# Prompt sparse attention: the order of transpositions, scores and values on TensorE

## The chip, the cores and the metric

The kernel runs on one core of a Trainium2 chip. The metric is the time of one execution in microseconds on the device, the median of several runs.

## What is computed

One inference step of a decoder layer for a prompt of 1024 tokens and 32 sample tokens, all in float32. The change lies in the prompt's native sparse attention. For 8 query heads in 2 key groups, cut to what matters:

```python
s = einsum(q, k) * DH ** -0.5 - slope * dist      # masked where not valid
e = exp(s - max(s)); p = e / sum(e)
# three branches over blocks of 128 queries:
#   compressed: up to 63 compressed keys (63 = 1024 // 16 - 1)
#   selected:   the 16 best blocks of 64 keys, here all causal keys
#   window:     the last 512 keys
o_a = g0 * o_compressed + g1 * o_selected + g2 * o_window
```

`g0` to `g2` are sigmoid gates. The rest of the layer (projections, a state-space mixer, dilated attention, cross attention, a feed-forward network) isn't touched.

## The kernel before

The program is a row of stages. A stage is a call of `together`, which takes lanes. A lane holds one generator per engine and a number of steps, and `together` writes the lanes' instructions engine by engine in an order set by numbers: step k of a lane that starts at `start` and takes `length` stands at `start + (k + 0.5) * length / steps`. So the order on each engine is fixed when the program is built, and lanes meet on an engine only in that order.

The stage of this case has four lanes: `dense.lane(36)`, start 0, length 1; `nsa_prompt_lane`, start 0.08, length 0.92; `branch_weights_lane`, start 0.3, length 0.3 (a few small operations); and `copies_lane`, which issues cache copies from ScalarE. The dense lane has 36 units of 8 steps, so 288, and a step is one gate matmul at L288 (two records in the trace, 352 columns); after a unit ScalarE or VectorE copies its output (L308). Matmuls in float32 show as two records each, transpositions as one.

`nsa_prompt_lane` first turns (transposes) 12 loaded groups of query and key rows (L644, `nsap_raw`; the loads are issued at L847 by SyncE, four groups deep). Then it has 32 attention steps s: 4 query heads r per key group times 8 query blocks i. A step works on both key groups g at once:

- **score** (L658): matmuls of `q_T` and `k_T` into the two buffers `nsap_S`, one per key group, in units of at most 512 columns. Units of step s+2 are made during step s.
- **bias** (L764, VectorE): adds the distance table, writes `nsap_probs`, and takes the maximum into `nsap_tops`; it releases the `nsap_S` buffer for the next unit. After the last unit `shift` (L775 to L778) makes `nsap_neg`.
- **exp** (L731, ScalarE): the exponential of a branch of step s+1, with its sum.
- **weight** (L784 to L791, VectorE): six multiplications of step s+1's probabilities by gate over sum.
- **turn_probs** (L644, TensorE): four (or two) transpositions of a group of `nsap_probs` into `nsap_T0` or `nsap_T1`; **copy_probs** (L706 on ScalarE, L708 on VectorE) takes them to `nsap_probs_T`, four groups deep, by the group's parity.
- **values** (L677): matmuls with `nsap_v` or `nsap_vcs` into `nsap_O`; after a step's last group ScalarE copies it to `nsap_oa` (L749).

A group is two 128-key tiles of both key groups, or the compressed keys. Step i has 2, 3, 4, 5, 6, 7, 7, 8 groups. `subs(s)` says how many sections (turns between which other lanes come) a step has. Section j of TensorE holds unit j of step s+2, the turn of group j and the values of group j-1:

```python
for j in range(subs(s)):
    if j < n_units(s + 2):
        score(s + 2, j)
    if j < n_groups(s):
        turn_probs(s, j)
    if 1 <= j <= n_groups(s):
        values(s, j - 1)
    yield
```

Of the kernel before, what the change touches and what calls it, by code (L numbers as in the profile page):

```python
# [23 lines left out]
P = 128  # L24
# [520 lines left out]
def nsa_prompt_lane(nc, st, ins, proj, kc_T, vc, oa_T, ident):  # L545
# [39 lines left out]
    def n_cmp(i):  # L585
        return min(NCMP_P, (i + 1) * P // CMP_S - 1)

    def units(i):
# [8 lines left out]
        out, width = [], 512  # L597
        for part in sel + win + [("cmp", 0, n_cmp(i), TX + 8 * (PT - 1 - i), CX, 4)]:
# [32 lines left out]
    def subs(s):  # L631
        return max(n_units(s + 2), n_groups(s) + 1, 3)
# [6 lines left out]
    def pe_program(pe):  # L639
# [49 lines left out]
        for s in range(2):  # L689
            for j in range(n_units(s)):  # L690
                score(s, j)
            yield
        for s in range(n):
            for j in range(subs(s)):
                if j < n_units(s + 2):
                    score(s + 2, j)
                if j < n_groups(s):
                    turn_probs(s, j)
                if 1 <= j <= n_groups(s):
                    values(s, j - 1)  # L700
                yield

# [13 lines left out]
    def copy_probs(eng, s, j, side):  # L716
        group = group0[s] + j
        if j < n_groups(s) and group % 2 == side:
# [6 lines left out]
    def act_program(act):  # L725
# [14 lines left out]
        yield  # L740
        for s in range(n):
            for j in range(subs(s)):
                copy_probs(act, s, j, 0)
                if s + 1 < n and j < 3:
                    exp(s + 1, (1, 2, 0)[j])
                if j == subs(s) - 1:
                    r, i = steps[s]
                    act.wait_ge(pv, group0[s + 1] - group0[0])
                    act.copy(oa[:, r, i * P:(i + 1) * P], O[s % 2][:, :]).then_inc(out_made, 1)  # L749
                yield  # L750

    def dve_program(dve):
# [51 lines left out]
        for s in range(n):  # L804
            for j in range(subs(s)):
                copy_probs(dve, s, j, 1)
# [4 lines left out]
                if j == subs(s) - 1 and s + 1 < n:  # L811
                    weight(s + 1)
                yield

    def pool_program(pool):
# [11 lines left out]
        for s in range(n):  # L827
# [5 lines left out]
            for _ in range(subs(s)):  # L833
                yield
# [4 lines left out]
    def sp_program(sp):  # L839
# [26 lines left out]
        for s in range(n):  # L866
# [4 lines left out]
            for _ in range(subs(s)):  # L871
                yield
# [4 lines left out]
    return Lane(len(preps) + 2 + sum(subs(s) for s in range(n)), pe_program, act_program, dve_program, pool_program, sp_program)  # L877
# [3243 lines left out]
```

## Time and profile before

| | before |
|---|---|
| median of 3 runs | 3273.9 us |
| lowest and highest run | 3272.72, 3279.45 us |
| profiled execution: span | 3273.0 us |
| TensorE busy | 3015.6 us, 92% |
| VectorE busy | 1257.5 us, 38% |
| ScalarE busy | 640.6 us, 20% |
| DMA | 344.79 MB, mean 105 GB/s |

The profile is of one execution. The span runs from its first to its last instruction; what lies around it is not in the table, since the times of the runs were taken apart. In the views PE is TensorE's matmuls and PEld its weight loads, DVE is VectorE, ACT ScalarE, SP SyncE, and a "q" behind an engine is its queue of waits and DMA issues. Idle time stands with what ended it. Matmuls are pipelined, so the time of a matmul in a stream is read from one start to the next.

### The profile page before, as it was taken

Reading aid. Unit: us, or ns where it says so; the run is one execution under the profiler, and the core shown is the slowest. Engines: PE = TensorE matmul, PEld = TensorE weight load, DVE = VectorE, ACT = ScalarE, POOL = GpSimd, SP = SyncE. Lnnn points to the kernel's source line nnn. Section 1 sums busy time; section 2 is a strip of 40 time slices with the busy share of each in tenths; the row PEclk is TensorE's granted clock in tenths of the full one; section 3 lists DMA queues with packets and bytes.
Section 4 is the critical chain, followed back from the end, with each engine's and each line's share of the span. In section 5 each row is a group of like instructions: output and inputs, shape, how many; then the busy total and the mean of one; then the engine's idle time right before and its main releaser. Section 6 shows DMA issues by size and latency. Waiting matters only on the chain. (4 is left out here: it accounts for less than half of the span.)

```text
span 3273.0 us, 42944 instructions
## 1 busy us (share of the span) xinstructions
PE 3015.6 (92%) x15198; PEld 2004.1 (61%) x15198; DVE 1257.5 (38%) x2963; ACT 640.6 (20%) x1529; POOL 469.3 (14%) x351
## 2 busy tenths in 40 slices
PE   7999999989997899699899899899699999989998
PEld 5777777665555565454554565455488888874443
DVE  3111123225642675255555343133456656550000
ACT  2111000002220333233333221144311111110000
POOL 0001000004301432100000100011122332220000
PEclk8999999999998889899999999899799999999999
DMA  7544253428854432621110444200143333404010
GB/s 171 118 95 103 75 166 112 146 84 231 254 160 129 147 103 65 181 69 36 40 32 33 142 138 156 94 15 33 55 141 110 121 136 108 141 22 158 34 34 26
DMA packets 336639, 344.79 MB, mean 105 GB/s; under 512 B 60945, under 2 KB 305361, under 8 KB 335078
## 3 DMA queue, kind: packets, MB, share of 16 engines
q1 hardware_dynamic: 296730, 262.54, 27.6%
q10 hardware_dynamic: 39734, 79.98, 7.2%
q8 instruction: 103, 1.69, 0.2%
q14 instruction: 72, 0.59, 0.1%
HBM read 289.11 MB, written 110.01 MB: 122 GB/s over the span
## 5 line engine op out<-in xcount | busy, mean ns | idle before, releaser
L284 PE MATMUL d_ps<-d_w,mixer_u_T 128*128 128x288 f32 (+2 forms) x2048 | 610.8, 437 | 15.9 <-PEq L145 10.3
L284 PEld LDWEIGHTS d_ps<-d_w,mixer_u_T 128*128 128x128 f32 x2048 | 375.4, 195 | 150.4 <-issue 47.9
L288 PE MATMUL d_ps<-mixer_u_T,d_w 128*128 128x352 f32 x1152 | 428.9, 498 | 24.4 <-ACT d_ob L308 13.8
L2923 PE MATMUL down_ps<-down_w,feed_g_T 128*128 128x512 f32 x704 | 305.4, 596 | 8.4 <-DMA down_w<-ffn_w_down 8.4
L288 PEld LDWEIGHTS d_ps<-mixer_u_T,d_w 128*128 128x128 f32 x1152 | 206.4, 199 | 131.8 <-issue 70.1
L2923 PEld LDWEIGHTS down_ps<-down_w,feed_g_T 128*128 128x128 f32 x704 | 134.4, 191 | 177.7 <-issue 168.5
L3133 PE MATMUL ffn_ps<-up_u_T,up_up_w 128*128 128x264 f32 x704 | 165.2, 394 | 6.3 <-DMA ffn_state<-state_ffn_conv 6.3
L3133 PE MATMUL ffn_ps<-up_u_T,ffn_S 128*128 128x264 f32 x704 | 163.8, 386 | 0.0
L3133 PE MATMUL ffn_ps<-ffn_T,up_up_w 128*128 128x264 f32 x704 | 163.8, 386 | 0.0
L308 DVE COPY d_ob<-d_ps 128x288 f32<-128x288 f32 (+3 forms) x144 | 66.4, 462 | 233.0 <-PE d_ps L284 158.3
L3133 PEld LDWEIGHTS ffn_ps<-up_u_T,up_up_w 128*128 128x128 f32 x704 | 133.8, 193 | 29.5 <-issue 6.7
L3133 PEld LDWEIGHTS ffn_ps<-up_u_T,ffn_S 128*128 128x128 f32 x704 | 133.8, 190 | 22.9
L3133 PEld LDWEIGHTS ffn_ps<-ffn_T,up_up_w 128*128 128x128 f32 x704 | 133.8, 190 | 22.9
L2763 PE MATMUL mix_B<-gates_o_T,mix_wb 128*128 128x352 f32 x480 | 144.1, 464 | 0.0
L3483 PE MATMUL tail_ps_a<-feed_g_T 128*128 128x512 f32 (+1 forms) x288 | 135.9, 622 | 6.1 <-DVE tail_y_a L3513 4.2
L2763 PEld LDWEIGHTS mix_B<-gates_o_T,mix_wb 128*128 128x128 f32 x480 | 92.1, 192 | 51.5 <-issue 1.5
L1320 PE MATMUL cmp_H<-cmp_rows_T,cmp_w 128*128 128x254 f32 (+1 forms) x576 | 122.6, 373 | 0.0
L3189 DVE TENSOR_TENSOR ffn_h<-ffn_kept,ffn_ps 128x264 f32<-128x264 f32 (+2 forms) x220 | 76.3, 372 | 120.6 <-PE ffn_ps L3133 117.8
L3252 DVE SCALAR_TENSOR_TENSOR ffn_c<-ffn_h,ffn_now,ffn_c 128x1072 f32<-128x1072 f32 x88 | 117.5, 1335 | 3.1
L764 DVE CUSTOM_DVE_ANT_0 nsap_probs<-nsap_S,nsap_scaled 128x128 f32<-128x128 f32 (+11 forms) x256 | 99.7, 435 | 43.6 <-PE nsap_S L658 43.6
L708 DVE COPY nsap_probs_T<-nsap_T 128x512 f32<-128x512 f32 (+4 forms) x84 | 53.6, 639 | 162.1 <-PE nsap_T L644 159.7
L1320 PEld LDWEIGHTS cmp_H<-cmp_rows_T,cmp_w 128*128 128x128 f32 x576 | 106.9, 196 | 14.3
(467 smaller groups left out, 3783.0 us busy)
## 6 DMA issues: line engine op xcount, KB each, us to landing
out_dil_sample<-cache_dil_w ACTq DMA_DIRECT2D x10, 3264.0 KB
up_up_w<-ffn_w_up SPq DMA_DIRECT2D x44, 512.0 KB, 5.1
cmp_rows<-cache_nsa_kv SPq DMA_DIRECT2D x128, 128.0 KB
graw<-d_ob SPq DMA_DIRECT2D x72, 176.0 KB
mix_gate<-graw SPq DMA_DIRECT2D x24, 528.0 KB, 6.0
dils_qb<-proj SPq DMA_DIRECT2D x24, 512.0 KB, 6.9
d_w<-w_in SPq DMA_DIRECT2D x24, 512.0 KB, 5.4
ssd_x<-proj SPq DMA_DIRECT2D x29, 384.0 KB, 4.8
```

Source lines behind the costliest of these rows:

```text
L284: mm = pe.matmul(self.ps[u % 2][0:rows, 0:cols], self.u_T[:, k, r0:r0 + rows], self.view(i)[:, k, :], start=(k == 0), stop=(k == DK - 1))
L288: mm = pe.matmul(self.ps[u % 2][:, 0:cols], self.view(i)[:, k, x, :], self.u_T[:, k, c * third:(c + 1) * third], start=(k == 0), stop=(k = ...
L308: copy(self.ob[0:rows, u % ring, 0:cols], self.ps[u % 2][0:rows, 0:cols]).then_inc(self.copied[u % 2], 1)
L708: eng.tensor_copy(out, src).then_inc(copied[1], 1)
L764: mm = dve.tensor_tensor_reduce(probs[:, s % 3, g, p0:p0 + b - a], S[g][:, col:col + b - a], scaled[:, r % 2, g, c0:c0 + b - a], 1.0, -3.0 ...
L1320: mm = pe.matmul(H[s][:, :, 0:blocks], w1[:, s, l, :], rows_T[:, r0:r0 + (KVH - 1) * LP + 1:LP, j:j + blocks], start=(l == 0), stop=(l == ...
L2763: mm = pe.matmul(B[u % BANKS][:, 0:third], wb[:, s, k, :], o_T[:, k, c * third:(c + 1) * third], start=(k == lo), stop=(k == hi - 1))
L2923: mm = pe.matmul(ps[i % ring][:, 512 * h:512 * (h + 1)], lhs_T[:, k, r0:r0 + m], w[:, k, 512 * h:512 * (h + 1)], start=(k == 0), stop=(k = ...
L3133: mm = pe.matmul(bank(p, x)[:, 0:quarter], lhs(slot)[:, k, :], rhs(x)[:, k, :], start=(k == 0), stop=(k == KH - 1))
L3189: dve.tensor_tensor(out, a, b, ALU.add).then_inc(summed, 1)
L3252: dve.scalar_tensor_tensor(out, row[:, k:k + conv], now[:, k, a:a + 1], out, ALU.mult, ALU.add).then_inc(convolved, 1)
L3483: mm = pe.matmul(ps_a[0:m, 512 * h:512 * (h + 1)], mix_T[:, k, r0:r0 + m], w_out[:, k, 512 * h:512 * (h + 1)], start=(k == 0), stop=(k == ...
```

## The change

- `units` packs a step's parts by size: the parts are sorted, the widest first, and each goes into the first unit with room. There are 88 units in all where there were 96.
- A section of TensorE now holds two groups' transpositions, then one score unit, then the values of both groups of the section before. `sections(s)` is the largest of the units of s+2, the pairs of groups, and 3.
- ScalarE does two of the three branches' exponentials in section 1, and the output copy (`take_out`) moves to the section in which the step's last values are made, which may be the first of the next step.
- VectorE weights step s+1 in the last section ahead of that section's biasing.
- The lane has 127 steps where it had 214.

```diff
+        for part in sorted(sel + win + [("cmp", 0, n_cmp(i), TX + 8 * (PT - 1 - i), CX, 4)], key=lambda x: x[1] - x[2]):
             m = part[2] - part[1]
-            if width + m > 512:
-                out.append([])
-                width = 0
-            out[-1].append((width, part))
-            width += m
+            for unit in out:
+                col, last = unit[-1]
+                at = col + last[2] - last[1]
+                if at + m <= 512:
+                    unit.append((at, part))
+                    break
+            else:
+                out.append([(0, part)])
...
-    def subs(s):
-        return max(n_units(s + 2), n_groups(s) + 1, 3)
+    def sections(s):
+        return max(n_units(s + 2), n_pairs(s), 3)
+    def n_pairs(s):
+        return (n_groups(s) + 1) // 2
+    def whole_at(s, j):
+        if j == 0 and s >= 1 and n_pairs(s - 1) == sections(s - 1):
+            return s - 1
+        return s if j == n_pairs(s) else None
+    def pair_of(s, j):
+        return range(2 * j, min(2 * j + 2, n_groups(s)))
...
+        before = []
         for s in range(n):
-            for j in range(subs(s)):
+            for j in range(sections(s)):
+                for x in pair_of(s, j):
+                    turn_probs(s, x)
                 if j < n_units(s + 2):
                     score(s + 2, j)
-                if j < n_groups(s):
-                    turn_probs(s, j)
-                if 1 <= j <= n_groups(s):
-                    values(s, j - 1)
-                yield
+                for x in before:
+                    values(*x)
+                before = [(s, x) for x in pair_of(s, j)]
+                yield
...
+            for j in range(sections(s)):
+                for x in pair_of(s, j):
+                    copy_probs(act, s, x, 0)
+                if s + 1 < n and j < 2:
+                    for br in ((1,), (2, 0))[j]:
+                        exp(s + 1, br)
+                if whole_at(s, j) is not None:
+                    take_out(whole_at(s, j))
+                yield
...
+                for x in pair_of(s, j):
+                    copy_probs(dve, s, x, 1)
+                if j == sections(s) - 1 and s + 1 < n:
+                    weight(s + 1)
                 if j < n_units(s + 2):
                     bias(s + 2, j)
                     if j == n_units(s + 2) - 1:
                         shift(s + 2)
-                if j == subs(s) - 1 and s + 1 < n:
-                    weight(s + 1)
                 yield
```

How the order moves, on TensorE, in the middle of step s=4 (i=4). Before:

```order
L658 MATMUL nsap_S<-nsap_k_T,nsap_q_T 128x512 x2
L644 MATMUL nsap_T<-const_ident,nsap_probs 128x128 x4
L677 MATMUL nsap_O<-nsap_probs_T,nsap_v 64x128 x4
L288 MATMUL d_ps<-mixer_u_T,d_w 128x352
L658 MATMUL nsap_S<-nsap_k_T,nsap_q_T 128x128 x2
L658 MATMUL nsap_S<-nsap_kc,nsap_q_T 128x55 x2
L644 MATMUL nsap_T<-const_ident,nsap_probs 128x128 x4
L677 MATMUL nsap_O<-nsap_probs_T,nsap_v 64x128 x4
L288 MATMUL d_ps<-mixer_u_T,d_w 128x352
L644 MATMUL nsap_T<-const_ident,nsap_probs 128x128 x4
L677 MATMUL nsap_O<-nsap_probs_T,nsap_v 64x128 x4
L288 MATMUL d_ps<-mixer_u_T,d_w 128x352
```

And now, where L661 is the transposition, L675 the score, L694 the values (counts here are matmuls of the program):

```order
L661 MATMUL nsap_T<-const_ident,nsap_probs 128x128 x8
L675 MATMUL nsap_S<-nsap_k_T,nsap_q_T 128x512 x2
L694 MATMUL nsap_O<-nsap_probs_T,nsap_vcs 64x128 x2
L694 MATMUL nsap_O<-nsap_probs_T,nsap_v 64x128 x4
L288 MATMUL d_ps<-mixer_u_T,d_w 128x352 x2
L661 MATMUL nsap_T<-const_ident,nsap_probs 128x128 x8
L675 MATMUL nsap_S<-nsap_k_T,nsap_q_T 128x384 x2
L675 MATMUL nsap_S<-nsap_k_T,nsap_q_T 128x128 x2
L694 MATMUL nsap_O<-nsap_probs_T,nsap_v 64x128 x8
L288 MATMUL d_ps<-mixer_u_T,d_w 128x352 x3
L675 MATMUL nsap_S<-nsap_kc,nsap_q_T 128x55 x2
L694 MATMUL nsap_O<-nsap_probs_T,nsap_v 64x128 x8
```

Each section had its own run of four transpositions and of four value matmuls; now eight stand together, twice as many gate matmuls follow, and the units of 512, 128 and 55 columns and of 384 columns are cut as 384 with 128, and 55 alone.

On VectorE, at the end of step s=3 (i=3). Before:

```order
L775 TENSOR_TENSOR nsap_tops<-nsap_tops 128x2x2
L777 TENSOR_SCALAR nsap_neg<-nsap_tops 128x2x2
L778 TENSOR_SCALAR nsap_neg<-nsap_tops 128x2
L708 COPY nsap_probs_T<-nsap_T 128x512
L784 SCALAR_TENSOR_TENSOR nsap_rs<-nsap_sums,nsap_eg 128x6
L786 RECIPROCAL nsap_rs<-nsap_rs 128x6
L791 TENSOR_SCALAR nsap_probs<-nsap_probs,nsap_rs 128x39 x2
L791 TENSOR_SCALAR nsap_probs<-nsap_probs,nsap_rs 128x640 x4
L764 ISA nsap_probs,nsap_tops<-nsap_S,nsap_scaled 128x512
L764 ISA nsap_tops 128x1
```

And now, with the weighting at L814 to L821 and the biasing at L794:

```order
L730 COPY nsap_probs_T<-nsap_T 128x512
L814 SCALAR_TENSOR_TENSOR nsap_rs<-nsap_sums,nsap_eg 128x6
L816 RECIPROCAL nsap_rs<-nsap_rs 128x6
L821 TENSOR_SCALAR nsap_probs<-nsap_probs,nsap_rs 128x39 x2
L821 TENSOR_SCALAR nsap_probs<-nsap_probs,nsap_rs 128x640 x4
L794 ISA nsap_probs,nsap_tops<-nsap_S,nsap_scaled 128x256
L794 ISA nsap_tops 128x1
L794 ISA nsap_probs,nsap_tops<-nsap_S,nsap_scaled 128x128
L794 ISA nsap_tops 128x1
```

The biasing and the shift of step 5's last unit stood ahead of the weighting of step 4; now the weighting follows the section's copy directly and the biasing comes behind it.

## Rows read from the trace of the kernel before

**Rows 1.** The page of the profile, its first part: busy time by engine.
```profile
PE 3015.6 (92%) x15198; PEld 2004.1 (61%) x15198; DVE 1257.5 (38%) x2963; ACT 640.6 (20%) x1529; POOL 469.3 (14%) x351
```

**Rows 2.** Windows: us, then each engine's busy time, granted clock, DMA share, GB/s.
```profile
1310.00:1860.00 550.00, 479.31 (x2960) 272.96 (x2960) 258.16 (x966) 183.53 (x533) 26.94 (x9) 0.97 0.22 65
...
1430.00:1460.00 30.00, 28.13 (x193) 16.13 (x194) 17.61 (x57) 9.95 (x26) 6.73 (x2) 1.00 0.10 31
...
1580.00:1590.00 10.00, 8.65 (x45) 5.62 (x46) 4.88 (x21) 7.59 (x16) 0.00 (x0) 0.66 0.48 125
```

**Rows 3.** Groups by line, 1325:1855: shapes, count | busy us, mean ns | idle before, releasers.
```profile
L644 PE MATMUL nsap_T<-const_ident,nsap_probs 128*128 128x128 f32 (+7 forms) x592 | 97.6, 283 | 3.4 <-DVE nsap_probs L791 3.4
L677 PE MATMUL nsap_O<-nsap_probs_T,nsap_v 128*64 128x128 f32 x1056 | 87.9, 286 | 4.0 <-ACT nsap_probs_T L706 3.6 <-DVE nsap_probs_T L708 0.4
L658 PE MATMUL nsap_S<-nsap_k_T,nsap_q_T 64*128 64x512 f32 (+3 forms) x384 | 83.0, 514 | 28.9 <-DVE nsap_tops L764 28.5
...
L658 PE MATMUL nsap_S<-nsap_kc,nsap_q_T 64*128 64x7 f32 (+7 forms) x128 | 11.5, 247 | 11.1 <-DVE nsap_tops L764 11.1
L644 PE MATMUL nsap_T<-const_ident,nsap_raw 128*128 128x128 f32 x48 | 9.8, 341 | 14.7 <-DMA nsap_raw<-proj 13.7 <-ACT nsap_k_T L706 1.0
```

**Rows 4.** Time line of PE: start, us, line, names, shapes, count [idle before].
```profile
1433.78 0.60 PE L644 MATMUL nsap_T<-const_ident,nsap_probs 128*128 128x128 f32 x4
1434.31 0.66 PE L677 MATMUL nsap_O<-nsap_probs_T,nsap_v 128*64 128x128 f32 x8
1434.90 0.86 PE L288 MATMUL d_ps<-mixer_u_T,d_w 128*128 128x352 f32 x2
1435.59 0.60 PE L644 MATMUL nsap_T<-const_ident,nsap_probs 128*128 128x128 f32 x4
...
1439.47 1.13 PE L658 MATMUL nsap_S<-nsap_k_T,nsap_q_T 64*128 64x512 f32 x4
1440.53 0.42 PE L644 MATMUL nsap_T<-const_ident,nsap_probs 128*47 128x128 f32 x2
...
1442.19 1.13 PE L658 MATMUL nsap_S<-nsap_k_T,nsap_q_T 64*128 64x512 f32 x4 [0.66 <-DVE nsap_tops L764]
1443.26 0.66 PE L644 MATMUL nsap_T<-const_ident,nsap_probs 128*128 128x128 f32 x4
1443.84 0.44 PE L677 MATMUL nsap_O<-nsap_probs_T,nsap_vcs 47*64 47x128 f32 x4
1444.21 0.86 PE L288 MATMUL d_ps<-mixer_u_T,d_w 128*128 128x352 f32 x2
```

**Rows 5.** The same view of PE while the loaded rows are transposed.
```profile
1353.03 0.76 PE L288 MATMUL d_ps<-mixer_u_T,d_w 128*128 128x352 f32 x2
1353.62 0.60 PE L644 MATMUL nsap_T<-const_ident,nsap_raw 128*128 128x128 f32 x4
1354.06 1.35 PE L288 MATMUL d_ps<-mixer_u_T,d_w 128*128 128x352 f32 x4
```

**Rows 6.** Time line of DVE over the end of the same step.
```profile
1436.30 0.69 DVE L708 COPY nsap_probs_T<-nsap_T 128x512 f32<-128x512 f32 x1 [1.70 <-PE nsap_T L644]
...
1437.32 2.38 DVE L791 TENSOR_SCALAR nsap_probs<-nsap_probs,nsap_rs 128x47 f32<-128x47 f32 x6
1440.74 0.69 DVE L764 CUSTOM_DVE_ANT_0 nsap_probs<-nsap_S,nsap_scaled 128x512 f32<-128x512 f32 x1 [1.03 <-PE nsap_S L658]
```

**Rows 7.** Groups of DVE by form, 1370:1850: one weighting of two widths.
```profile
L791 DVE TENSOR_SCALAR nsap_probs<-nsap_probs,nsap_rs 128x640 f32<-128x640 f32 x40 | 19.8, 547 | 0.0
...
L791 DVE TENSOR_SCALAR nsap_probs<-nsap_probs,nsap_rs 128x1024 f32<-128x1024 f32 x8 | 5.6, 747 | 0.0
```

**Rows 8.** Time lines of SP's queue and of PE at the first steps.
```profile
1343.92 12.06 SPq L847 DMA_DIRECT2D nsap_raw<-proj  x14
...
1370.50 0.61 PE L658 MATMUL nsap_S<-nsap_kc,nsap_q_T 64*128 64x15 f32 x4 [4.43 <-DVE nsap_tops L764]
```

**Rows 9.** Time line of PE at the longest wait inside the loop.
```profile
1581.35 0.70 PE L677 MATMUL nsap_O<-nsap_probs_T,nsap_v 128*64 128x128 f32 x4 [3.56 <-ACT nsap_probs_T L706]
```

More of the change, by code:

```diff
@@ L692, in pe_program @@
             yield
+        before = []
         for s in range(n):
[L694 removed]
+            for j in range(sections(s)):
+                for x in pair_of(s, j):
+                    turn_probs(s, x)
                 if j < n_units(s + 2):
                     score(s + 2, j)
[L697 to L700 removed]
+                for x in before:
+                    values(*x)
+                before = [(s, x) for x in pair_of(s, j)]
                 yield
+        for x in before:
+            values(*x)
+        yield
     def copy_group(eng, group, out, src):
@@ L717, in copy_probs @@
         group = group0[s] + j
-        if j < n_groups(s) and group % 2 == side:
+        if group % 2 == side:
             pairs = blocks(steps[s][1])[j]
@@ L740, in act_program, with take_out @@
         yield
+        def take_out(s):
+            r, i = steps[s]
+            act.wait_ge(pv, group0[s + 1] - group0[0])
+            act.copy(oa[:, r, i * P:(i + 1) * P], O[s % 2][:, :]).then_inc(out_made, 1)
         for s in range(n):
[L742 to L749, printed above, removed]
+            for j in range(sections(s)):
[6 more added lines that the diff above has]
+                    take_out(whole_at(s, j))
                 yield
+        if n_pairs(n - 1) == sections(n - 1):
+            take_out(n - 1)
+        yield
     def dve_program(dve):
@@ L804, in dve_program @@
         for s in range(n):
-            for j in range(subs(s)):
-                copy_probs(dve, s, j, 1)
+            for j in range(sections(s)):
+                for x in pair_of(s, j):
+                    copy_probs(dve, s, x, 1)
+                if j == sections(s) - 1 and s + 1 < n:
+                    weight(s + 1)
                 if j < n_units(s + 2):
@@ L832, in pool_program @@
                 scale(r + 1)
-            for _ in range(subs(s)):
+            for _ in range(sections(s)):
                 yield
@@ L870, in sp_program @@
                 sp.dma_start(oa_T[r - 1], oa[:, r - 1, :]).then_inc(stored, 16)
-            for _ in range(subs(s)):
+            for _ in range(sections(s)):
                 yield
@@ L875, in sp_program @@
         sp.wait_ge(stored, 16 * NSA_R)
-    return Lane(len(preps) + 2 + sum(subs(s) for s in range(n)), pe_program, act_program, dve_program, pool_program, sp_program)
+    return Lane(len(preps) + 2 + 1 + sum(sections(s) for s in range(n)), pe_program, act_program, dve_program, pool_program, sp_program)
 def dil_prompt_lane(nc, st, ins, proj, o_dil, od_T, ident):
```

3 lines of the change are left out of this document (1 added, 2 removed).

## The prediction

> **What bounds the kernel now.** The page first: TensorE is busy for 92% of the span and no other engine for more than 38% [rows 1]. So the questions are how long the stage that the change touches lasts, and what TensorE does there. The windows give its place: from about 1327 us (first transposition of nsap_raw) to 1849.5 us; of the 550 us that hold it TensorE shows 479 busy, VectorE 258, ScalarE 184, the DMA engines 22% [rows 2]. In the first 60 us TensorE waits for loads; afterwards it is busy for 26 to 29 of every 30 us at a granted clock of 1.00, as in 1430:1460.
>
> The groups by line then say what ends the idle time [rows 3]: 40.0 us before score matmuls (28.9 + 11.1), for VectorE's biasing of the unit before; 14.7 us before the transpositions of loaded rows, for DMA; 3.4 us for the weighting; 4.0 us before value matmuls, 3.6 of it a single event. That is 47.4 us without the loads.
>
> The time line of TensorE shows a second loss, which counts as busy [rows 4, 5]. Four transpositions (T) take 0.44 us from start to start if a gate matmul (D) follows, 0.53 us if values (V) follow: 0.09 for leaving. One D (two records) takes 0.59 us after a T, 0.70 after a V (0.69 in the rounded rows): 0.11 for entering. I take 0.09 for leaving a D too. A V of 8 records takes 0.59 us and one of 4 takes 0.37: 0.055 for a record, so 0.15 us of any V run is fixed. A 512-wide score unit (S) takes 1.06 us against 0.85 at D's rate of 0.59 us per 352 columns: 0.20. T after S takes 0.58 where T after D takes 0.53: 0.05. T and D have the same shape of weights, 128*128, S has 64*128 and V 128*64; with like shapes nothing is lost, with every other neighbour about 0.16 us.
>
> **The change, part by part.** No matmul, copy, exponential or byte is removed or added; only order and waits move.
>
> *Fewer changes of shape.* I counted runs of one kind from the first transposition of the stage to its end in the built order. Before there are 657 runs: 170 D entered from V or S (0.11 each, 18.7 us), 127 D left to S or V (0.09, 11.4), 95 S runs (0.20, 19.0), 93 T after S (0.05, 4.7), 136 T left to V (0.09, 12.2) and 168 V runs (0.15, 25.2): 91.2 us. After there are 406: 111 entered (12.2), 19 left (1.7), 87 S (17.4), no T after S, 92 T left (8.3), 92 V (13.8): 53.4 us. The difference is **-38 us**. Two neighbours, T before S and S before V, are nearly absent before; I take leaving and entering as above, and bound each at 0.05 either way, +-7 us over some 137 of them.
> The Trainium skill, in TensorEngine Tiling (Array Packing), Key Properties, says that a change of tiling mode drains the engine. Read as a wait until the last matmul has ended (the 283 ns that a transposition takes), the 236 changes removed would be worth 67 us and the time would be 3176 us; the start-to-start times above have no room for that, and the measured 0.16 us decides.
>
> *Score units wait for less.* Now a unit is biased in one section and the next is scored after only V and one D, while VectorE needs 2.72 us from a 512-wide unit's start to its release: 1.27 us until it begins, two biasings of 0.65, 0.15 to wake TensorE [rows 4, 6]. After the change S, V8, D2, T8 stand between (numbers now count the program's matmuls: V4 is 8 records, a second V4 adds 0.44): 1.05 + 1.03 + 1.29 + 0.96 = 4.3 us. VectorE's copy of the section lies within the 1.27 us, so inside a step these waits go. The packing by size takes 96 units down to 88, so 8 fewer such waits; it moves no column.
>
> *A new wait at the end of a step.* VectorE now weights step s+1 in the last section ahead of that section's biasing, behind its copy, and TensorE's next transpositions need it; then the next score needs the biasing behind it. A weighting takes 2.7 us from the copy's end [rows 6], for widths 768, 640 and 47; two widths' durations [rows 7] give 0.067 us for 128 columns, so 3.0 for step i=7, 2.85 for 6, 2.6 for 4. The copy starts 0.71 us after the first transposition and takes 0.69 [rows 4, 6]. Step by step, TensorE's path from the last T to the next against VectorE's, without and with a copy of its own:
> i=6: T4 0.53 + V8 1.03 + D2 1.29 = 2.85, against 0.7 (1.4) + 3.0 + 0.15 = 3.85 (4.55): 1.0 to 1.7 us lost.
> i=3: with a 431-column unit 3.8 against 3.45 (4.15), and then two biasings, taken at the 0.65 us of 512 columns, before the next score: 0.4 to 1.0.
> i=5: two transpositions alone, 3.15 against 3.5 (4.0): 0.35 to 0.85. i=7 and 0: 0 to 0.5. i=1, 2, 4 have a last section without transpositions, which covers it: 0.
> The middles make 3.1 us a round of eight steps, 12.4 us for four. Behind the waiting transposition stand on TensorE the gate matmuls, which nobody needs soon. I keep the first steps' wait of 4.43 us [rows 8] (it hangs on the chain bias, exponential, weighting of step 0, which isn't touched) and the 4.0 us before values, though their cover grows. Stalls: 47.4 - 12.4 - 4.4 - 4.0, **-27 us**. Bounds: boundaries 0 to 25 us (twice the middles), -39 to -14.
>
> *ScalarE* gets two branches' exponentials in a section (about 2.4 us with the longest copy 3.0) against sections of 3 to 4.3 us, and its output copy moves up to a section later; O is double-buffered, so the cost is nothing. Should ScalarE be late, T would wait for its buffer first.
>
> *Loads.* The lane's 214 turns become 127 beside the same 288 gate matmuls, so each gets 2 or 3 D instead of 1 or 2; the twelve turns with loads get ten D more. SyncE issues the loads in its order: 14 between 1343.92 and 1355.98 us [rows 8], so they land no earlier; but the waits take in gate matmuls. The ten D are 5.9 us; from 0 to 9 us of the 14.7 [rows 3]: **-4.5 us**.
>
> The sum: -38 - 27 - 4.5 = -69 us. The profiled execution has a span of 3273.0 us, the median of the three runs is 3273.9, so against the median **3205 us**, 2.1% less.
>
> **The rivals.**
> *The boundary costs more.* If VectorE's tail takes 1.75 us at all 31 boundaries, 54 us, the gain is 38 + 4.5 + 47.4 - 54 - 8.4 = 27 us: 3246 us. For it: everything that VectorE does is in one queue, and the copy ahead of the weighting waits for TensorE itself. Against it: four of eight steps have the spare section or little to weight. Chance 0.12.
> *Waits inside a run.* Each run of T8 or V8 holds a semaphore wait in its middle; 76 joins of T and 76 of V. If each stops the early load of weights, at the 0.11 us that D pays for it: 17 us, 3222 us. Against it: a T with a wait behind a D costs nothing now (0.59). Chance 0.08.
> *The clock (slower than before).* Around the 3.56 us wait that ends at 1581.35 us [rows 9] the window 1580:1590 has a granted clock of 0.66 [rows 2], 6.8 us at 1.2 GHz in place of 2.4: 3.4 us of work lost. If every boundary, with its wait and a run of transpositions on either side, did the same, 31 x 3.4 = 105 us: 3310 us, slower; it decides from 20 drops on. Against it: the window 1430:1460 has 1.00 [rows 2] though TensorE waits in it (0.66 us at 1442.19 [rows 4]). Chance 0.04.
> The Trainium skill, in TensorE: Matmul & The Clock Gate, Part 4, PE-mode transpose, says that transpositions don't count as busy for the clock, which speaks against gathering them; the trace, where that window has transpositions in every turn and 1.00, shows no sign of it so far.
> *The change does nothing.* If gate matmuls and not the waits set the pace, all would move and nothing shrink: 3274 us. The 40 us of named waits speak against it. Chance 0.02.
>
> **How the numbers follow.** My forecast has 0.74. Its own bounds: gains of 31 + 14 + 0 = 45 to 45 + 39 + 9 = 93, the ends unlikely together. With the joins inside and the boundary rival half inside, 3186 to 3240 us. Faster than before by over 0.2% (about what a measurement can tell here, 6.5 us): 0.94; within: 0.02; slower: 0.04.
>
> **What would show it.** After: idle before the score matmuls under 15 us, before transpositions for the weighting 8 to 15 us, in steps i=6, 3 and 5; 406 runs with the same start-to-start prices (T8 before S 0.96 us, V8 before D 1.03); the last value matmul about 1780 us; loads' waits about 10 us; granted clock 1.00 in the stage's windows. I am wrong if T before S or S before V costs over 0.25 us, if idle before transpositions passes 30 us, or if windows fall below 0.9.

## The result, and the profile after

The changed kernel has a median of 3198.5 us (3192.5 to 3199.9, four runs), the kernel before on the same chip 3275.1 us: a ratio of 0.976 [0.9744, 0.9776], 76.6 us less. Forecast were 3205 us and 69 us less; the range held the time. A second measurement of the same kernel beside the experiments gave 0.977 [0.9748, 0.9792]. One execution, of e5 below, took 8313.6 us at a mean granted clock of 0.57 and is left out of its median.

The page of the changed kernel, the span and the busy times, which answer to [rows 1]:

```profile
span 3198.0 us, 42937 instructions
...
PE 2970.8 (93%) x15198; PEld 2010.5 (63%) x15198; DVE 1260.8 (39%) x2963; ACT 639.6 (20%) x1529; POOL 469.7 (15%) x351
```

The count of matmuls is the same, 15198, yet TensorE's busy time fell by 44.8 us: what a change of shape costs is counted as busy, as the prediction had read it, and so is what the lower clock costs (both are taken apart below). The other 30 us of the span's 75.0 were idle time. The windows of the stage, with the columns of [rows 2], show how full TensorE is now:

```profile
1310.00:1790.00 480.00, 443.04 (x2970) 284.49 (x2972) 261.40 (x969) 182.98 (x534) 29.33 (x11) 0.97 0.26 77
...
1430.00:1460.00 30.00, 29.38 (x214) 19.14 (x214) 21.26 (x71) 13.31 (x34) 6.73 (x2) 1.00 0.10 18
```

In 1430:1460 it was busy for 28.13 us with 193 matmul records; now for 29.38 with 214. The groups by line from 1325 to 1780 us answer to [rows 3]:

```profile
L661 PE MATMUL nsap_T<-const_ident,nsap_probs 128*128 128x128 f32 (+7 forms) x592 | 80.7, 275 | 7.3 <-DVE nsap_probs L821 6.6 <-DVE nsap_probs_T L730 0.6
L694 PE MATMUL nsap_O<-nsap_probs_T,nsap_v 128*64 128x128 f32 x1056 | 78.0, 281 | 0.0
L675 PE MATMUL nsap_S<-nsap_k_T,nsap_q_T 64*128 64x512 f32 (+3 forms) x384 | 77.9, 499 | 2.3 <-DVE nsap_tops L794 2.3
L675 PE MATMUL nsap_S<-nsap_kc,nsap_q_T 64*128 64x7 f32 (+7 forms) x128 | 11.4, 253 | 4.4 <-DVE nsap_tops L794 4.4
L661 PE MATMUL nsap_T<-const_ident,nsap_raw 128*128 128x128 f32 x48 | 9.2, 325 | 12.8 <-DMA nsap_raw<-proj 12.8
```

The waits before scores went from 40.0 to 6.7 us, and 4.4 of those are the single wait at the first steps. The waits before values are gone. Those of the transpositions for the weighting rose from 3.4 to 6.6 us; those for loads hardly moved, 13.7 to 12.8.

**The stage by its parts.** The same reading was made of every kernel below, from the first transposition of nsap_raw to the last value matmul. The columns are the stage's length; the number of runs of one kind in the order, and their price by the prediction's start-to-start prices (91.2 and 53.4 us there; a sum over every neighbour gives 90.4 and 52.9, and this one sum is used for all kernels); TensorE's waits before scores, before transpositions for the weighting, for loads, and before values; and the time in it at the lower clock of 1.2 GHz. All in us except the runs.

Each row is read from one profiled execution. The whole times of one kernel differ by up to 18 us from run to run, and the profiled execution was the fastest or nearly the fastest of its kernel for e3, e5 and e7 and the slowest for e2b and e8, so small differences between rows, those at 1.2 GHz above all, may be of the execution and not of the kernel. The changed kernel was profiled twice: its stage took 447.5 and 447.6 us, with 23.9 us at 1.2 GHz both times.

| kernel | stage | runs | price | scores | weighting | loads | values | at 1.2 GHz |
|---|---|---|---|---|---|---|---|---|
| before | 521.8 | 657 | 90.4 | 39.9 | 3.4 | 13.7 | 4.0 | 34.1 |
| after | 447.5 | 406 | 52.9 | 6.7 | 6.6 | 12.8 | 0 | 23.9 |
| e1_turn_first | 499.0 | 657 | 83.4 | 12.9 | 14.4 | 13.2 | 3.2 | 30.7 |
| e7_units_only | 509.4 | 649 | 87.7 | 35.9 | 3.4 | 11.6 | 4.0 | 23.9 |
| e8_branch_spread | 524.4 | 657 | 90.4 | 38.8 | 6.8 | 13.4 | 0.8 | 41.0 |
| e2b_alternate | 463.7 | 512 | 67.6 | 4.7 | 9.1 | 12.8 | 0 | 27.3 |
| e3_old_units | 449.7 | 422 | 56.1 | 4.4 | 7.1 | 13.1 | 0 | 23.9 |
| e4_weight_behind | 496.8 | 406 | 52.9 | 4.4 | 47.9 | 13.6 | 0 | 47.8 |
| e5_weight_ahead | 439.7 | 406 | 52.9 | 4.8 | 1.6 | 13.5 | 0 | 23.9 |

Before to after: price -37.5, waits for VectorE and ScalarE from 47.3 to 13.3, -34.0, loads -0.9, and 10.2 us less at half speed, worth half of that if TensorE had work throughout, -5.1 (an estimate). That makes -77.5 us; the stage shrank by 74.3, and of the span's 75.0 all but 0.7 lies in it. Two small waits stand in no column: the 1.0 us for ScalarE's copy of nsap_k_T [rows 3] is gone, and 0.6 us for VectorE's copy to nsap_probs_T is new.

### The profile page after: what moved, and what is told of

Its sections match the earlier page's. It is cut to its first block and busy times, and to the rows that moved or that the text cites. A ratio compares the mean times of both kernels' runs of the same rounds, so it can differ in the third digit from the quotient of the medians.

```text
span 3198.0 us, 42937 instructions
## 1 busy us (share of the span) xinstructions
PE 2970.8 (93%) x15198; PEld 2010.5 (63%) x15198; DVE 1260.8 (39%) x2963; ACT 639.6 (20%) x1529; POOL 469.7 (15%) x351
## 3 DMA queue, kind: packets, MB, share of 16 engines
q8 instruction: 103, 1.69, 0.2%
## 5 line engine op out<-in xcount | busy, mean ns | idle before, releaser
L288 PE MATMUL d_ps<-mixer_u_T,d_w 128*128 128x352 f32 x1152 | 404.3, 489 | 24.8 <-ACT d_ob L308 14.2
L794 DVE CUSTOM_DVE_ANT_0 nsap_probs<-nsap_S,nsap_scaled 128x512 f32<-128x512 f32 (+11 forms) x256 | 99.5, 438 | 39.9 <-PE nsap_S L675 39.9
L753 ACT ACTIVATE nsap_probs<-nsap_probs,nsap_neg 128x640 f32<-128x640 f32 (+9 forms) x192 | 112.6, 589 | 11.4 <-DVE nsap_neg L808 11.4
```

The source lines that it names most:

```text
L288: mm = pe.matmul(self.ps[u % 2][:, 0:cols], self.view(i)[:, k, x, :], self.u_T[:, k, c * third:(c + 1) * third], start=(k == 0), stop=(k = ...
L753: act.activation(x, x, ACT.Exp, scale=DH ** -0.5, bias=neg[:, s % 3, g, br:br + 1], accum_out=sums[:, s % 3, g, br:br + 1]).then_inc(exped, 1)
L794: mm = dve.tensor_tensor_reduce(probs[:, s % 3, g, p0:p0 + b - a], S[g][:, col:col + b - a], scaled[:, r % 2, g, c0:c0 + b - a], 1.0, -3.0 ...
```

## The experiments

Ten edits, most of them one piece of code each, were made from the kernel before or from the changed one; the ratio is always to the kernel before on the same chip, in runs beside it.

**e1: the order of a section alone.** From the kernel before: transpositions ahead of the score, four at a time, and nothing else.

```diff
+                if j < n_groups(s):
+                    turn_probs(s, j)
                 if j < n_units(s + 2):
                     score(s + 2, j)
-                if j < n_groups(s):
-                    turn_probs(s, j)
                 if 1 <= j <= n_groups(s):
                     values(s, j - 1)
```

> The kernel before, still one group a section, with the transpositions ahead of the score unit instead of behind it. My theory: what ends the waits before scores is that transpositions, values and a gate matmul lie between a score unit and the next while VectorE's copy no longer stands behind the score: 1.06 + 0.59 + 0.69 + 0.53 = 2.9 us against the 2.72 us that VectorE needs. Idle before score matmuls falls from 40.0 to about 12 us, the changes of shape cost 83 us instead of 90, so about 35 us less than before: 3240 us. Rival: the waits go only with two groups and two gate matmuls in a section; then only the 7 us of shapes are gained: 3268 us.

Measured: 3245.0 us, 0.9916 [0.989, 0.9943], 26.7 us less. The groups by line from 1320 to 1825 us:

```profile
L644 PE MATMUL nsap_T<-const_ident,nsap_probs 128*128 128x128 f32 (+7 forms) x592 | 93.7, 276 | 14.4 <-DVE nsap_probs L791 14.4
...
L658 PE MATMUL nsap_S<-nsap_k_T,nsap_q_T 64*128 64x512 f32 (+3 forms) x384 | 82.5, 513 | 6.9 <-DVE nsap_tops L764 6.5
...
L658 PE MATMUL nsap_S<-nsap_kc,nsap_q_T 64*128 64x7 f32 (+7 forms) x128 | 11.4, 251 | 6.0 <-DVE nsap_tops L764 6.0
```

The order by itself gives the score its cover: 39.9 to 12.9 us of waits. But the weighting, which here still stands behind the biasing, then holds up transpositions that come earlier: 3.4 to 14.4 us. So of 27 us won 11 are given back, for which the expectation had no term; its 3240 us was 5 us too fast. The move of the weighting in the change is meant for this, and e4 tests it.

**e7: the packing of the units alone.** From the kernel before, with the new `units` (the first hunk of the change's diff).

> The kernel before with only the packing by size: 88 units instead of 96. My theory: 8 score waits fewer at about 0.75 us and 2.7 us less of changes of shape, together 8 us: 3267 us. Rival: the packing merges columns into units that are biased longer and wait longer, so nothing comes of it: 3275 us.

Measured: 3263.9 us over ten runs, 0.9971 [0.9955, 0.9986], 7.8 us less than the 3271.7 beside it. The groups by line from 1320 to 1835 us:

```profile
L661 PE MATMUL nsap_S<-nsap_k_T,nsap_q_T 64*128 64x512 f32 (+3 forms) x384 | 78.8, 502 | 24.8 <-DVE nsap_tops L767 24.8
...
L661 PE MATMUL nsap_S<-nsap_kc,nsap_q_T 64*128 64x7 f32 (+7 forms) x128 | 11.8, 257 | 11.1 <-DVE nsap_tops L767 11.1
```

Eight units fewer are eight waits and eight runs fewer: 4.0 us less waiting before scores, 2.7 us of price. Together 6.7 us, near the 7.8 of the whole program. The stage is 12.4 us shorter in the trace, with 2.1 us less waiting for loads and 10.2 us less at 1.2 GHz; but the profiled execution, 3258.1 us, was 6 us faster than the median, so these last terms can't be put down to the packing.

**e3: the changed kernel with the old packing.** The same hunk undone.

> The changed kernel with the packing by size undone: 96 units again. 422 runs of one kind instead of 406, 56.1 us of changes of shape instead of 52.9, and i=4 to 6 have 4 units each, so the steps two ahead of them get a fourth section with a single score unit. My theory: the waits of score units are covered in either case, so only the 3 us of shapes are lost: 3202 us. Rival: the packing is what took the waits away; then 8 or more waits of 0.75 us come back: 3208 us.

Measured: 3200.3 us, 0.978 [0.9761, 0.98], against 3197.6 and 0.977 for the changed kernel in the same runs; the stage is 2.2 us longer. Price +3.2, waits before scores -2.3, before transpositions +0.5, loads +0.3: 1.7. The packing was worth 8 us where each unit had a wait, and some 2 us, less than these runs can resolve, once the waits were covered.

**e2b: the same waits, more changes of shape.** From the changed kernel: in a section each group's transpositions stand directly ahead of one of the two value groups, and the score last. This keeps two groups in a section, the lane's steps, and VectorE's and ScalarE's programs as they are.

```diff
-                for x in pair_of(s, j):
-                    turn_probs(s, x)
+                pair = list(pair_of(s, j))
+                for at in range(2):
+                    for x in pair[at:at + 1]:
+                        turn_probs(s, x)
+                    for x in before[at:at + 1]:
+                        values(*x)
                 if j < n_units(s + 2):
                     score(s + 2, j)
-                for x in before:
-                    values(*x)
```

> The changed kernel, its sections as they are, but inside a section the two groups alternate: transpositions, values, transpositions, values, then the score unit. 512 runs of one kind instead of 406; by the prices of the prediction 67.6 us of changes of shape instead of 52.9. My theory: 15 us slower than the changed kernel, 3213 us, with waits as they are (under 4 us of difference). Rival: the gain came from waits alone and runs of one kind are worth nothing: 3198 us.

Measured: 3215.7 us, 0.9814 [0.9785, 0.9843]; the stage is 16.2 us longer than the changed kernel's. By the table: price +14.7, waits +0.5, 3.4 us more at half speed +1.7, 16.9 in all. Against the two measurements of the changed kernel the whole program's ratio is 0.0044 to 0.0054 higher, 14 to 18 us. So the price of a change of shape, which had been read from pairs of neighbours, holds as a sum over 106 runs. The time line of TensorE (the columns of [rows 4]) in e2b shows what the price consists of:

```profile
1477.56 0.60 PE L661 MATMUL nsap_T<-const_ident,nsap_probs 128*128 128x128 f32 x4
1478.09 0.44 PE L694 MATMUL nsap_O<-nsap_probs_T,nsap_vcs 63*64 63x128 f32 x4
1478.46 0.65 PE L661 MATMUL nsap_T<-const_ident,nsap_probs 128*128 128x128 f32 x4
1479.04 0.66 PE L694 MATMUL nsap_O<-nsap_probs_T,nsap_v 128*64 128x128 f32 x8
```

Four transpositions take 0.53 and then 0.58 us from start to start (0.44 in a stream), although nothing waits. That the weights' shape is what costs, and not something else in which these kinds of matmul differ, is read from the neighbours: transpositions and gate matmuls differ in all but that shape and lose nothing. No run varies the shape alone.

**e4: the weighting behind the biasing.** From the changed kernel, on VectorE alone.

```diff
-                if j == sections(s) - 1 and s + 1 < n:
-                    weight(s + 1)
                 if j < n_units(s + 2):
                     bias(s + 2, j)
                     if j == n_units(s + 2) - 1:
                         shift(s + 2)
+                if j == sections(s) - 1 and s + 1 < n:
+                    weight(s + 1)
```

> The changed kernel with VectorE's weighting of step s+1 behind the last section's biasing, where it stood before. My theory: the weighting ends 1.3 to 2.3 us later in the steps i=1, 2, 3 and 5, where the last section has a score unit; about 7.6 us in a round of eight steps, 30 us in four: 3227 us, as idle time before transpositions that wait for the weighting. Rival: VectorE has time enough (busy for 55% of the stage) and its order doesn't matter: 3198 us.

Measured: 3245.8 us, 0.9917 [0.9888, 0.9947]: of the 76 us only 26 remain. Waits for the weighting are 47.9 us in place of 6.6, and the stage is 49.3 us longer; the waits make 39 us of that (41.3 more, 2.3 fewer before scores). The expectation, 3227 us, was 19 us too fast: it had the direction and 30 us of waits. Most of the rest goes with the clock. The time line of TensorE behind one such wait:

```profile
1464.51 1.53 PE L661 MATMUL nsap_T<-const_ident,nsap_probs 128*55 128x128 f32 x6 [7.44 <-DVE nsap_probs L821]
...
1470.48 1.69 PE L661 MATMUL nsap_T<-const_ident,nsap_probs 128*128 128x128 f32 x8
```

Eight transpositions take 1.69 us here, and 1.04 in the changed kernel. The windows of e4 and of the changed kernel, from 1380 us to each stage's end:

```profile
1380.00:1825.00 445.00, 397.07 (x2726) 250.15 (x2722) 251.84 (x917) 171.83 (x505) 13.46 (x4) 0.97 0.13 39
```

```profile
1380.00:1775.00 395.00, 385.42 (x2720) 245.56 (x2718) 247.34 (x917) 171.44 (x502) 13.46 (x4) 1.00 0.15 43
```

The granted clock is 0.97 against 1.00, 47.8 us of the stage at 1.2 GHz against 23.9. That is worth at most 12 us, and 8 if only the time counts in which TensorE was busy at the lower clock; the stage leaves room for 10.

Not all of these waits are the price of the weighting's place. There are 24, one at each end of a step in which the transpositions need the weighting; at i=5 the wait is 7.44 us in the first two rounds and 1.87 in the other two. In the first two GpSimd works beside VectorE, from 1455.66 and from 1571.56 us, 6.73 us each time. The time line of VectorE there, in the first round and then in the third:

```profile
1455.79 3.27 DVE L807 TENSOR_SCALAR nsap_neg<-nsap_tops 128x4 f32<-128x4 f32 x1
...
1459.36 5.10 DVE L821 TENSOR_SCALAR nsap_probs<-nsap_probs,nsap_rs 128x55 f32<-128x55 f32 x6
```

```profile
1688.58 2.52 DVE L821 TENSOR_SCALAR nsap_probs<-nsap_probs,nsap_rs 128x55 f32<-128x55 f32 x6
```

So 2 x 5.57, 11 us of the 41, come from VectorE held beside GpSimd (the last section is on that), and the two longest stretches at 1.2 GHz in the loop, 10.2 us each, begin at 1461.6 and 1577.6 us, inside these two waits. Without GpSimd's work the place of the two lines would cost about 30 us of waits, an estimate from the third and fourth rounds, which is what had been expected.

**e5: the weighting ahead of the copy.** The other way from e4: the two lines `if j == sections(s) - 1 ...: weight(s + 1)` stand ahead of the section's `copy_probs`.

> The changed kernel with VectorE's weighting of step s+1 ahead of the last section's copy, so that it need not wait for TensorE's transpositions first. My theory: the chain behind the copy makes the waits that are left before transpositions (7.2 us with 1.44 us in each of four steps i=6) and 2.4 us of those before scores; without the copy in front most of them go: 3198 - 8 = 3190 us. Rival: the copy, now late by up to 3 us, holds back values or the next transpositions by as much: 3198 us or more.

Measured: 3192.8 us, the middle of three runs, 0.9743 [0.9719, 0.9767]; the interval overlaps the changed kernel's, so by the times alone the gain isn't shown. The trace has what was expected: waits for the weighting 6.6 to 1.6 us, before scores 6.7 to 4.8, stage 7.8 us shorter. In the groups by line:

```profile
L661 PE MATMUL nsap_T<-const_ident,nsap_probs 128*128 128x128 f32 (+7 forms) x592 | 80.7, 274 | 2.4 <-DVE nsap_probs L821 1.6 <-DVE nsap_probs_T L730 0.8
```

The weighting needs only ScalarE's exponentials, the copy needs the section's transpositions; with the copy first, VectorE waits for TensorE before it does work that TensorE will wait for.

**e8: the single wait before values.** The kernel before had one wait of 3.56 us before values [rows 9] with a drop of the clock around it. Its chain led back to the lane of the branches' weights. From the kernel before, that lane is spread, so that its ScalarE step comes one turn later:

```diff
+        yield
         act.wait_ge(small, 4)
...
+        yield
         dve.wait_ge(small, 5)
...
-    return Lane(4, None, act_program, dve_program, pool_program, sp_program)
+    return Lane(6, None, act_program, dve_program, pool_program, sp_program)
```

> The kernel before with two more turns in the lane of branch weights, so that ScalarE and VectorE don't wait for one another in the same turn. My theory: ScalarE's wait of 6.4 us there held the copy that the values waited for (3.56 us), and the low clock from 1580.8 to 1587.6 us followed from that wait: both go, 3.6 + 3.4 = 7 us: 3268 us. Rival: the low clock there has another cause: only 3.6 us: 3271 us, and the low stretch is still in the trace.

Measured: 3276.0 us over ten runs, 0.9998 [0.9986, 1.0011]: the same. Both the theory and the rival had forecast a gain. The wait went (values 4.0 to 0.8 us) and so did the drop beside it, but others came, and waits for the weighting rose by 3.4. The windows of e8 at the old place and at a new one:

```profile
1520.00:1530.00 10.00, 8.66 (x35) 4.28 (x36) 3.53 (x12) 2.62 (x9) 0.00 (x0) 0.66 0.06 19
...
1580.00:1600.00 20.00, 17.92 (x131) 11.40 (x130) 14.01 (x39) 8.54 (x19) 6.73 (x2) 1.00 0.24 64
```

The low stretch of 6.8 us from 1522.9 us stands behind waits of 0.68, 1.01, 0.50 and 1.29 us, so a drop needs no single long wait. With about 40 us of waits before scores still spread over the stage, the drops moved and their sum did not fall in the one execution profiled: 41.0 us at 1.2 GHz here, 34.1 before. What decides their places stays open.

The waits for the weighting rose because VectorE was still held beside GpSimd (the last section), now with the weighting's first instruction in the place of the lane's:

```profile
1585.94 2.76 DVE L784 SCALAR_TENSOR_TENSOR nsap_rs<-nsap_sums,nsap_eg 128x6 f32<-128x6 f32 x1
```

It takes 0.17 us in the kernel before at 1579.03 us. TensorE then waits 1.50 us for this weighting at 1591.54; a second such wait, 1.43 us at 1608.27, isn't explained here.

**e6, e6b: where the lane stands beside the gate matmuls.** Ahead of the stage TensorE has gate matmuls of the dense lane; the prompt lane's turns lie between the shares 0.08 and 0.92 of it. A later start gives the loads more time.

```diff
-(nsa_prompt_lane(nc, own, ins, proj, kc_T, vc, oa_T, ident), 0.08, 0.92)
+(nsa_prompt_lane(nc, own, ins, proj, kc_T, vc, oa_T, ident), 0.12, 0.88)
```

e6b has 0.16, 0.84 in the same place.

> The changed kernel with the attention lane placed at 0.12 of the stage instead of 0.08, so 11 or 12 gate matmuls (6.8 us) more stand ahead of the first transposition of loaded rows. My theory: the loads are issued by SyncE at their own pace, so these matmuls fill the waits of 3.64 and 9.12 us: 6.8 us and some of the low clock around them: 3190 us. Rival: the loads' order stands behind the lane's turns in SyncE's queue and moves with them, nothing is filled: 3198 us.

> The same with 0.16: 23 gate matmuls (13.5 us) more ahead of the first transposition. My theory: the waits for loads (12.8 us) are nearly gone and the clock stays at 2.4 GHz through the loads: 12 us and 5 us, 3182 us. Rival: each further load waits for the turn four groups before it, so waits of about 5 us a load group remain, whatever stands ahead: 3190 us.

Measured: e6 3190.5 us, 0.9743 [0.9714, 0.9773], as expected, with an interval that overlaps the changed kernel's; e6b 3211.0 us, 0.9793 [0.9771, 0.9814], slower than its theory (3182) and its rival (3190). The time line of TensorE in e6, with one wait for loads where the changed kernel has two:

```profile
1347.22 1.12 PE L661 MATMUL nsap_T<-const_ident,nsap_raw 128*128 128x128 f32 x4 [8.65 <-DMA nsap_raw<-proj]
```

The first wait, 3.64 us, is gone; the second, 9.12, is still 8.65. The time at 1.2 GHz fell from 23.9 to 17.1 us. (The stage itself isn't comparable for these two, since fewer gate matmuls fall into it.) In e6b, 0.04 later again, something else waits. Its time lines, TensorE and ScalarE:

```profile
1357.43 1.51 PE L288 MATMUL d_ps<-mixer_u_T,d_w 128*128 128x352 f32 x2 [9.19 <-ACT d_ob L308]
...
1383.40 1.11 PE L661 MATMUL nsap_T<-const_ident,nsap_raw 128*128 128x128 f32 x4 [9.38 <-DMA nsap_raw<-proj]
```

```profile
1356.84 0.45 ACT L308 COPY d_ob<-d_ps 128x352 f32<-128x352 f32 x1 [22.75 <-DMA graw<-d_ob]
```

A gate matmul waits 9.19 us for ScalarE's copy of an earlier one, and that copy had waited 22.75 us for the store of its buffer to land. SyncE's queue, which issues both, was taken by one load (nsap_eg) from 1322.36 us for 18.99 us and came to these stores only at 1351.33. So the dense lane's stores and the prompt lane's loads are tied through SyncE, and moving the lane trades one wait for another: of the three places tried, 0.12 gave the lowest time.

**e9: e5 and e6 together.**

> The changed kernel with both edits that helped: VectorE's weighting ahead of the last section's copy, and the attention lane at 0.12 of the stage. My theory: the two gains lie in different places (boundaries of steps, loads) and add up: 6 + 8 us, 3184 us. Rival: with the lane later a unit's output copy meets the loads, or the low clock moves into the loop: 3190 us, no better than one of them.

Measured: 3183.6 us, 0.9724 [0.9703, 0.9745], against 0.977 [0.9748, 0.9792] for the changed kernel in the same runs: 14.0 us less, and the intervals are apart. Its groups by line from 1325 to 1765 us:

```profile
L661 PE MATMUL nsap_T<-const_ident,nsap_probs 128*128 128x128 f32 (+7 forms) x592 | 80.4, 274 | 0.8 <-DVE nsap_probs_T L730 0.8
```

No transposition waits for the weighting any more. This is the lowest time measured; its interval overlaps those of e5 and e6, so it isn't settled that the two gains add up in full.

## Why the prediction was right, and where it was off

**The fewer changes of shape: -38 us forecast.** Right. The start-to-start times it named came back in the changed kernel. Its time line:

```profile
1409.79 1.04 PE L661 MATMUL nsap_T<-const_ident,nsap_probs 128*128 128x128 f32 x8
1410.76 1.13 PE L675 MATMUL nsap_S<-nsap_k_T,nsap_q_T 64*128 64x512 f32 x4
1411.82 0.43 PE L694 MATMUL nsap_O<-nsap_probs_T,nsap_vcs 31*64 31x128 f32 x4
1412.18 0.66 PE L694 MATMUL nsap_O<-nsap_probs_T,nsap_v 128*64 128x128 f32 x8
1412.77 1.45 PE L288 MATMUL d_ps<-mixer_u_T,d_w 128*128 128x352 f32 x4
1414.05 0.60 PE L661 MATMUL nsap_T<-const_ident,nsap_probs 128*128 128x128 f32 x4
...
1415.59 1.09 PE L694 MATMUL nsap_O<-nsap_probs_T,nsap_v 128*64 128x128 f32 x16
1416.62 1.45 PE L288 MATMUL d_ps<-mixer_u_T,d_w 128*128 128x352 f32 x4
```

Eight transpositions before a score take 0.97 us (0.96 forecast), sixteen value records before a gate matmul 1.03 (1.03), the gate matmuls before a transposition 1.28 (1.29), and a score before values 1.06, as a score before a transposition had been. So the neighbours that the trace of before nearly lacked, bounded by +-7 us in all, cost what the others do. e2b confirms the price from the other side. The rule of the Trainium skill that had been weighed beside it (TensorEngine Tiling (Array Packing), Key Properties: changing the tiling mode drains the engine) stays as it was read: with the price of a full drain the time would have been 3176 us, with the measured one 3205, and 3198.5 came out, of which the missing terms are found below. e2b is the sharper test: its 104 more neighbours of unlike shape would have cost 29 us at 283 ns each, and it is 14 to 18 us slower.

**The rival of waits inside a run** (17 us, 3222 us) is refuted by the same rows: the runs of eight and sixteen have a wait in their middle and cost nothing for it.

**The waits: -27 us forecast, -34 measured.** The mechanism was right and the term of the boundary was too large. Forecast were 12.4 us: 1.35 at i=6, 0.7 at i=3, 0.6 at i=5, the rest at i=7 and 0. Measured are 8.9 (6.6 before transpositions and 2.3 before scores): 1.44 or 1.45 at each of the four i=6, 0.60 before the score in three of four at i=3, nothing at i=5, and 0.33 and 0.50 at two others. Time line of TensorE at i=6, and of VectorE beside it:

```profile
1459.85 0.60 PE L661 MATMUL nsap_T<-const_ident,nsap_probs 128*128 128x128 f32 x4
1460.38 1.09 PE L694 MATMUL nsap_O<-nsap_probs_T,nsap_v 128*64 128x128 f32 x16
1461.40 1.45 PE L288 MATMUL d_ps<-mixer_u_T,d_w 128*128 128x352 f32 x4
1464.30 0.87 PE L661 MATMUL nsap_T<-const_ident,nsap_probs 128*63 128x128 f32 x6 [1.45 <-DVE nsap_probs L821]
```

```profile
1460.55 0.69 DVE L730 COPY nsap_probs_T<-nsap_T 128x512 f32<-128x512 f32 x1 [2.58 <-PE nsap_T L661]
...
1461.58 2.67 DVE L821 TENSOR_SCALAR nsap_probs<-nsap_probs,nsap_rs 128x63 f32<-128x63 f32 x6
```

The copy starts 0.70 us after the last four transpositions, the weighting ends at 1464.25, and TensorE goes on at 1464.30: 4.45 us on VectorE's path where the prediction had 3.85 without a copy of its own and 4.55 with one. VectorE did have the copy here, and the middle was taken; at i=5 it did not come to a wait at all. The rest of the difference is the 4.0 us before values, which had been kept and went: 3.56 of it because the branches' weights fall elsewhere in the new order.

**The loads: -4.5 us forecast, -0.9 measured.** This step failed. "The waits take in gate matmuls" holds only where the load's time is fixed and TensorE comes to the wait later by them. The small waits did take them in (4.32 to 3.64 us, and 0.35 and 1.78 to nothing), but the long one grew from 7.23 to 9.12. The loads are issued by SyncE in the program's order, and in this stretch it is its queue that sets their time. SyncE's queue in the changed kernel:

```profile
1316.65 13.08 SPq L883 DMA_DIRECT2D nsap_eg<-proj  x1
...
1340.70 4.16 SPq L250 DMA_DIRECT2D graw<-d_ob  x3
1344.91 5.32 SPq L878 DMA_DIRECT2D nsap_raw<-proj  x8
```

and TensorE's wait for a load of this block, in the kernel before and now:

```profile
1348.91 1.11 PE L644 MATMUL nsap_T<-const_ident,nsap_raw 128*128 128x128 f32 x4 [7.23 <-DMA nsap_raw<-proj]
```

```profile
1349.84 1.12 PE L661 MATMUL nsap_T<-const_ident,nsap_raw 128*128 128x128 f32 x4 [9.12 <-DMA nsap_raw<-proj]
```

The block that began at 1343.92 us [rows 8] now begins at 1344.91, 1.0 us later, behind the dense lane's weights and stores, and TensorE left the wait 0.9 us later. It also reached it 1.0 us earlier, at 1340.72 where the kernel before had 1341.68, although three of the ten added gate matmuls stand ahead of it: the wait of 0.98 us for ScalarE's copy was gone, and the first low stretch of the clock ended at 1338.5 us where before it lasted to 1341.9. The other seven went into the turns behind it. The later lane of e6 takes 4.2 us of these waits away, so the term was to be had, by another edit.

**The clock: nothing forecast, about -5 us read.** In the kernel before two drops lay in the loop, 3.4 us from 1396.5 us and 6.8 us around the wait of [rows 9]; in the changed one TensorE has 1.00 from 1380 us to the stage's end, in both of its profiled executions. The prediction used that drop only as the price of a rival. The rival itself (3310 us, slower) did not come. The waits behind the first steps stayed at 1.45 us at most, but that this kept the clock up isn't shown: e2b, with the same waits at i=6, has a drop of 3.4 us just behind one of them. e4 shows that the rival was real in part: with 24 waits for the weighting, two of them 7.44 us and the others 2.25 or less, three drops come, at some 10 us in the sum and not at 105. The Trainium skill says, in TensorE: Matmul & The Clock Gate, Part 4, PE-mode transpose, that transpositions don't count as busy for the clock. Here eight of them stand together in most sections and the granted clock stays at 1.00 for 395 us, so at this share of transpositions the trace shows no loss by it; no run here has a stretch of transpositions alone.

**The dearer boundary** (54 us, 3246 us) did not come either. e4 comes to its sum, with 47.9 us of waits and 3245.8 us, once the weighting stands behind the biasing; so its place ahead is what kept most of these waits away, though 11 us of e4's are GpSimd's doing.

The terms measured add up to -77.5 us against -74.3 in the stage. The 3 us between them lie inside the bound of the shapes' term and can't be settled from these traces, in which some matmul records are missing. Against the forecast the waits gave 7 us more and the clock 5, the loads 4 less: that 3205 came as near as 6.5 us is owed in part to errors that cancel, and the clock's share of it is luck.

## What to carry to other kernels

Read TensorE's time line from start to start, by neighbours: 0.16 us at each change of the weights' shape is counted as busy and shows in no list of waits, and here it was half of the gain. When an order is changed to cover one engine's waits, write down what the other engine does between the last input and the release at every boundary, and put first in its queue the work that needs nothing of the engine it will be waited for by (e5 against e4: 0.9743 and 0.9917 of the kernel before, on the place of two lines, of which GpSimd and the clock have a share). And before counting on more cover for a load, look at whether its issue moves with the cover.

## What was not expected of the hardware

A tiny instruction of VectorE can last as long as one of GpSimd's. Twice among the attention steps GpSimd scales two tables; in the kernel before, at the second of these places:

```profile
1572.00 6.72 POOL L819 TENSOR_SCALAR nsap_scaled<-nsap_tab,nsap_slopes 128x1215 f32<-128x1215 f32 x2 [112.66 <-DVE nsap_tops L764]
```

```profile
1572.14 3.27 DVE L777 TENSOR_SCALAR nsap_neg<-nsap_tops 128x4 f32<-128x4 f32 x1
1575.63 2.87 DVE L2607 TENSOR_TENSOR const_lse<-const_lse,nsap_w_stats 128x108 f32<-128x108 f32 x1
```

The negation of 128x4 values takes 0.17 us elsewhere. Started 0.13 us behind GpSimd's, it takes 3.27, which with 0.13 before it is one of GpSimd's two (6.72 for both). The next one, 2.87 us, fills the rest of the second; in the changed kernel, with no GpSimd beside it, it takes 0.27. The same 3.27 us stand there in the changed kernel too, where the copy and the biasing that follow come late:

```profile
1549.88 3.27 DVE L807 TENSOR_SCALAR nsap_neg<-nsap_tops 128x4 f32<-128x4 f32 x1
```

and in e1, e7, e2b and e8 as well. At the first of its two places the changed kernel has one that starts in the middle of GpSimd's second:

```profile
1453.51 2.21 DVE L807 TENSOR_SCALAR nsap_neg<-nsap_tops 128x4 f32<-128x4 f32 x1
```

```profile
1448.97 6.73 POOL L850 TENSOR_SCALAR nsap_scaled<-nsap_tab,nsap_slopes 128x1215 f32<-128x1215 f32 x2 [98.54 <-DVE nsap_tops L794]
```

It ends at 1455.72 and GpSimd's pair at 1455.70: VectorE's time is whatever is left of GpSimd's. In the kernel before, the 3.56 us wait of [rows 9] comes from here: the held VectorE instructions make ScalarE wait 6.40 us for const_lse, its copy is late (it starts at 1580.95 us), and the values wait for the copy. ScalarE's time line:

```profile
1579.22 0.29 ACT L2599 ACTIVATE const_lse<-const_lse 128x108 f32<-128x108 f32 x1 [6.40 <-DVE const_lse L2611]
```

That link is read from the chain; no run takes GpSimd's work away. e8 and e4 bear it out: in e8 the wait before values goes when ScalarE's step moves, while VectorE is held about as long as before, and in e4, whose weighting comes behind the held negation, TensorE's wait is 5.57 us longer in just the two rounds with GpSimd's work. The Trainium skill says, in SBUF — State Buffer, SBUF: two separate sides, that VectorE and GpSimd share a pair of ports which one instruction holds for its whole length while the other fully blocks; by that rule a VectorE instruction that needs the pair would end when GpSimd's does, and these rows agree, with 3.27 us for 0.17. Biasings of VectorE (L794) that ran between 1452.33 and 1453.40 us beside that same work kept their usual times, and no run here shows why.
